# Head-by-head projection, a prefix-maximum scan and earlier attention units in the third mixer

## The reference

```python
z = u @ w_in                                  # q, k, v, o: 4 heads x 128 each; i, f: 4 each; rx, ry: 512 each
logf = log_sigmoid(f); b = cumsum(logf)       # over tokens
dmat[t, s] = b[t] - b[s] + i[s]               # s <= t, else -inf
m[t] = max(b[t] + m0, max_s dmat[t, s])       # m0 = 0: the running maximum
s[t, s] = (q @ k.T) * 128**-0.5 * exp(dmat - m)
h = (s @ v) / max(|sum_s s|, exp(-m))
y_a = sigmoid(o) * h
# the other half: causal conv of width 4 over rx, two gate matmuls, a linear recurrence
a = exp(-8 * r * softplus(-lam)); hr = scan(a, sqrt(1 - a**2) * (i_gate * xc))
y_b = gelu(ry) * hr
y = concat(y_a, y_b) @ w_out
```

## Time and profile before

| | us |
|---|---|
| median of 3 runs (2483.32 to 2484.29) | 2483.36 |
| the profiled execution | 2485.89 |
| its span | 2484.1 |
| PE busy | 2389.3 (96%) |
| DVE busy | 1200.3 (48%) |
| ACT busy | 1110.6 (45%) |
| POOL busy | 1030.5 (41%) |

### The profile page before, as it was taken

How to read it: one execution, slowest core, us unless ns; L and a number is a source line. 1 busy time by engine, 2 the same in 40 slices (tenths; PEclk the granted TensorE clock), 3 DMA queues, 4 the chain that set the end, 5 groups by cost and what they waited for, 6 DMA issues and landing times.

```text
span 2484.1 us, 40506 instructions
## 1 busy us (share of the span) xinstructions
PE 2389.3 (96%) x13254; PEld 1956.0 (79%) x13254; DVE 1200.3 (48%) x2391; ACT 1110.6 (45%) x2412; POOL 1030.5 (41%) x750
## 2 busy tenths in 40 slices
PE   7999999999999989988999999999898999999998
PEld 6878787877877768666888888887766888888886
DVE  5555455554677762564444522224775424522224
ACT  5433343444555554553644533323565644523332
POOL 4444444442533324432652544443412642544442
PEclk9999999999999999988999999999999999999999
DMA  5333333332332213221431333332322431333332
GB/s 186 114 101 94 102 91 103 101 102 94 105 91 85 85 52 102 71 65 63 127 108 52 95 101 94 96 95 74 90 65 77 132 102 52 111 94 93 101 92 77
DMA packets 126066, 232.01 MB, mean 93 GB/s; under 512 B 17120, under 2 KB 17248, under 8 KB 125920
## 3 DMA queue, kind: packets, MB, share of 16 engines
q1 hardware_dynamic: 123072, 219.56, 29.7%
q10 hardware_dynamic: 2848, 10.49, 1.2%
HBM read 208.48 MB, written 2.10 MB: 85 GB/s over the span
## 4 chain that ended last, share of the span: by engine, by line
issue 53%; PE 24%; POOL 21%; ACT 1%; DVE 1%; POOLq 1%; DMA 0%; ACTq 0%; DVEq 0%; SPq 0%
PE PS L440 22%; POOL wl L411 21%; PE PS L507 1%; PE PS L519 1%; PE PS L474 0%; DMA raw<-tiles_dram 0%; POOLq L410 0%; POOLq L419 0%; ACT wh L1102 0%; DVE H L1781 0%; PE PS L514 0%; ACT work L1211 0%; ACT work L1131 0%; DVE work L1718 0%; ACT work L1254 0%
## 5 line engine op out<-in xcount | busy, mean ns | idle before, releaser
L411 POOL TENSOR_TENSOR wl<-raw,wh 128x512 fp32r<-128x512 f32 x746 | 1030.3, 1404 | 1425.9 <-ACT wh L1102 1424.6
L440 PE MATMUL PS<-uh,wh 128*128 128x512 f32 (+1 forms) x2184 | 810.3, 371 | 13.5 <-ACT work L1254 4.6
L440 PE MATMUL PS<-uh,wl 128*128 128x512 f32 (+1 forms) x2184 | 793.7, 363 | 0.0
L440 PE MATMUL PS<-ul,wh 128*128 128x512 f32 (+1 forms) x2184 | 792.6, 363 | 0.0
L1102 ACT ACTIVATE wh<-raw 128x512 fp32r<-128x512 f32 x746 | 430.5, 623 | 348.3 <-PE PS L440 280.4
L440 PEld LDWEIGHTS PS<-uh,wh 128*128 128x128 f32 x2184 | 414.8, 190 | 99.2 <-issue 15.2
L440 PEld LDWEIGHTS PS<-uh,wl 128*128 128x128 f32 x2184 | 414.2, 190 | 65.1
L440 PEld LDWEIGHTS PS<-ul,wh 128*128 128x128 f32 x2184 | 415.1, 190 | 60.8 <-issue 1.0
L440 PE MATMUL PS<-wh,hid_sb 128*128 128x512 f32 x1024 | 322.1, 396 | 0.0
L1254 ACT ACTIVATE work<-PS 128x512 f32<-128x512 f32 (+1 forms) x156 | 89.7, 575 | 339.6 <-PE PS L440 271.2
L440 PEld LDWEIGHTS PS<-wh,hid_sb 128*128 128x128 f32 x1024 | 192.4, 188 | 46.1
(11 more groups left out here) (224 smaller groups left out, 2421.6 us busy)
## 6 DMA issues: line engine op xcount, KB each, us to landing
raw<-tiles_dram SPq DMA_DIRECT2D x746, 256.0 KB, 2.7
work<-work SPq DMA_DIRECT2D x296, 64.0 KB, 2.0
gB<-post_dram ACTq DMA_DIRECT2D x8, 512.0 KB, 3.7
H<-x_dram SPq DMA_DIRECT2D x4, 512.0 KB, 6.4
H<-x_dram ACTq DMA_DIRECT2D x4, 512.0 KB, 5.0
work<-mem_dram ACTq DMA_DIRECT2D x2, 1024.0 KB, 5.8
out_dram<-H ACTq DMA_DIRECT2D x4, 512.0 KB, 2.6
cst<-consts_dram SPq DMA_DIRECT2D x1, 644.0 KB, 5.2
```

The costliest lines, as they stand in the source:

```text
L411: nc.gpsimd.tensor_tensor(w_of(wl, slot)[:, hc], raw[:, s, hc], w_of(wh, slot)[:, hc].bitcast(F32), ALU.subtract).then_inc(lo_ready, 1)
L440: last = nc.tensor.matmul(out, a, b, start=start and m == 0, stop=stop and m == 2)
```

## The change

**Tile order.** After rx comes the tile of i and f (tile 4), then ry (5 to 8), then q, k, v, o of head 0 (9 to 12), of head 1 (13 to 16), and so on. The output projection's rows are reordered so that the recurrence's half comes first (`EV_HEADS`).

**Row maxima.** m[t] is the running maximum of i[s] - b[s], raised by b[t]: one scan with `max` over the 4 rows replaces 16 masked maxima over blocks. Only the 128x128 diagonal blocks need the mask, so they are added once into `diagonals` (16 instructions), and the exponential reads E or the diagonals directly, in two instructions per unit where n > 0.

**Units inside the tiles.** After tile m, TensorE now does the scores of unit m - 11, the transposes of unit m - 12 and the values of unit m - 13, each in one PSUM bank instead of two. Both barriers are gone. The pieces of the last units lie between pieces of the output projection (`begin`), which starts with the rows that are finished; 38 of its 64 row pieces come this way. The output gate is evacuated by a tanh directly, v at half scale.

**The recurrence** keeps its work, after tiles 5, 9, 13 and 17.

```diff
-RG_AFTER = [10, 14, 18, 22]
+RG_AFTER = [5, 9, 13, 17]
+EV_HEADS = [4, 5, 6, 7, 0, 1, 2, 3]
...
+                def ml_scores(k):
+                    h, n = k // 4, k % 4
+                    pe.wait_ge(lin_evac, LIN["ev"] + 11 + 4 * h)
+                    scores(U + k, [(PS[:, 4, 0:(n + 1) * P], eq(h)[:, n * P:(n + 1) * P], ek(h)[:, 0:(n + 1) * P],
+                                    True, True)])
...
+                    if m >= 11:
+                        ml_scores(m - 11)
+                    if m >= 12:
+                        ml_transposes(m - 12)
+                    if m >= 13:
+                        ml_values(m - 13)
...
+                begin(n, u_out, EV_EARLY[0:2], MOVED_MEM)
+                pe.wait_ge(aux_taken, AUX["ev"] + 4)
+                begin(n, u_out, EV_EARLY[2:5], MOVED_MEM)
+                ml_scores(14)
+                ml_transposes(13)
+                ml_values(12)
+                begin(n, u_out, EV_EARLY[5:10], MOVED_MEM)
...
+                    if m >= 10:
+                        ml_exps(m - 10)
+                    if m >= 12:
+                        ml_pt(m - 12)
...
-                for h in range(ML_H):
-                    nc.scalar.activation(eg[h], F[:, h, :], ACT.Tanh, scale=0.5)
...
+                    v.tensor_tensor_scan(gif[0:4, :], ones4[0:4, :], gtmp[1][0:4, :], 0.0, ALU.mult, ALU.max)
...
-                def ml_weights_max(k):
...
+                            v.tensor_tensor(eD(h)[:, ns], eA[h][:, ns], maskn[:, 384:512], ALU.add)
...
+                conv(0)
+                ml_rows()
+                gelu(0)
+                rg_gates(0)
+                rg_scan(0)
...
+                ml_probs(0)
+                conv(2)
+                gelu(2)
+                ml_values_in(0)
+                ml_probs(1)
+                rg_gates(2)
+                ml_probs(2)
+                rg_scan(2)
+                ml_probs(3)
```

More of the change, by code:

```diff
@@ L906, in _ @@
[L906 to L913, removed]
@@ L914, in _ @@
-                bound()
+                    if m >= 12 and m % 4 == 0:
+                        h = m // 4 - 3
+                        pe.wait_ge(lin_evac, LIN["ev"] + m)
+                        wait(pe, aux_taken, AUX["ev"] + h)
+                        for t in range(TT):
+                            last = nc.tensor.transpose(PS[:, 7, t * P:(t + 1) * P], evt[:, t * P:(t + 1) * P], ident)
+                        last.then_inc(aux_ready, 1)
+                    if m == 11:
+                        pe.wait_ge(act_step, 4)
@@ L1456, in rg_start, with ml_pt, head_hi @@
+                def ml_pt(k):
+                    w = (k % 4 + 1) * P
+                    pt(UNIT["ev"] + k, ept(k)[:, 0:w], PS[:, 5, 0:w])
+                def head_hi(p0, p1):
+                    for p in range(p0, p1):
+                        act.wait_ge(rows_read, c.get("rows") + min(p + 1, KT - 1))
+                        nc.scalar.activation(uh[:, p, :], F[:, EV_HEADS[p], :], ACT.Copy).then_inc(uh_ready, 1)
                 def rg_start(q):
@@ L2122, in _, with gelu @@
                     v.drain().then_inc(conv_ready, 1)
+                def gelu(q):
+                    dve.wait_ge(lin_evac, L0 + 6 + q)
                     v.tensor_tensor(gel, F[:, 4 + q, :], F[:, 4 + q, :], ALU.mult)
@@ L2189, in _ @@
[L2189 to L2201 removed]
+                    v.scalar_tensor_tensor(F[:, h, :], F[:, h, :], 1.0, PS[:, 6, :], ALU.add, ALU.mult)
@@ new lines, in ml_result, with head_lo @@
+                    v.drain().then_inc(y_taken, 1)
+                def head_lo(p0, p1):
+                    for p in range(p0, p1):
+                        dve.wait_ge(uh_ready, c.add("uh"))
+                        v.tensor_tensor(ul[:, p, :], F[:, EV_HEADS[p], :], uh[:, p, :].bitcast(F32), ALU.subtract)\
+                            .then_inc(u_ready, 1)
+                step()
+                conv(0)
[3 more added lines that the diff above has]
+                rg_scan(0)
@@ new lines, in _ @@
+                conv(1)
+                gelu(1)
+                ml_diagonals()
+                rg_gates(1)
+                rg_scan(1)
+                ml_probs(0)
[7 more added lines that the diff above has]
+                ml_probs(3)
+                conv(3)
+                gelu(3)
+                ml_probs(4)
+                ml_values_in(1)
@@ new lines, in _ @@
+                ml_probs(5)
+                ml_result(0)
+                rg_gates(3)
+                ml_probs(6)
+                rg_scan(3)
+                ml_probs(7)
+                ml_probs(8)
+                ml_values_in(2)
+                ml_probs(9)
+                ml_result(1)
+                ml_probs(10)
+                ml_probs(11)
+                ml_probs(12)
+                head_lo(0, 2)
+                ml_values_in(3)
+                ml_probs(13)
+                ml_result(2)
@@ L2408, in tok, with toks @@
         out.append(("t", w, row, at))
-    def toks(w):
+    def toks(w, rows=range(4)):
         for nb in range(2):
-            for j in range(4):
+            for j in rows:
                 tok(w, 256 * j, 512 * nb)
```

258 lines of the change are left out of this document (146 added, 112 removed).

## The result

The changed kernel takes 2444.27 us (median of 4 runs, 2441.51 to 2448.54), the kernel before on the same chip 2483.82 (4 runs): a ratio of 0.9842, 95% interval 0.9826 to 0.9857, 39.5 us less. Predicted were 2452.5 and 31 less, so the forecast was 8.2 too high; 2444.27 lies just inside the lower end of the stated range (2444). The profiled execution took 2441.51, its span is 2439.7 at a mean clock of 0.992, against 2484.1 at 0.982 before.

The account below looks back on a forecast made before the run. TensorE, busy 96% of the span, was taken to bound the kernel. Base -39.1 plus waits 8.2 gave -30.9: from the profiled 2485.89 to 2455.0, the median 2.53 lower, so 2452.5 us, range 2444 to 2467.

Parts of the forecast that it names:

- The base sum: Third mixer, if TensorE never waits: -31.4 for attention, -8.2 for the convolution hole, +0.5 for tiny transposes, -39.1 us.
- the 55.0 that go: The attention stretch without tile work, between the last turned head of v and the output projection, disappears: 55.0 us.
- the 23.6 that come back: Attention matmuls returning between the tiles: 22.0 us at full clock, plus 1.6 for changing between kinds of matmul.
- the 8.2 of the hole: First gate matmuls' wait for VectorE's convolution, 4.26 us, goes, with slow clock of 1.95 and 2.0: together -8.2.
- The waits: TensorE waiting for VectorE and ScalarE in the new order: 8.2 us in sum, between 2.9 and 13.
- rival (B): The waits vanish, each bound falling low: 2447.2 us, or 2444.3 with none at all; chance 0.14.
- the main case: Waits of 4 to 14 us including some lower clock, giving 2448 to 2459 us; chance 0.62.
- units 2 and 6 (1.2 each): VectorE's work for these units stands behind the gates of recurrence blocks 2 and 3, so TensorE waits 1.2 us each.
- Rival (A): GpSimd blocks VectorE and the relay paces TensorE: 14 us more, 2466.5; chance 0.18 with what resembles it.
- The predicted -31.4: Net of the attention stretch: 55.0 us removed, 23.6 us of matmuls and changeovers added between the tiles.
- wrong, if the rhythm is 8 and more: Sign against the prediction: per-tile rhythm of 8 us and more, where 6.4 to 7.5 was expected.
- Rival (C): Slower than before: waits between tiles keep TensorE at its lower clock, up to 2487 us; chance 0.06 with other slow mishaps.

Follow-up runs that it names:

- e8: The changed kernel run again unchanged, with a second profile: 2443.9 us, ratio 0.9841.
- e5: The changed kernel with the gate matmuls of recurrence blocks 2 and 3 behind the unit's work, VectorE in that order too: 2443.6 us.
- e1: The kernel before with only the first convolution moved ahead of the row work on VectorE: 2475.8 us, ratio 0.9973.
- e10: The kernel before with both the scan and its diagonals and the first convolution ahead of the row work, heads still alone behind barriers: 2463.3 us.
- e7: The changed kernel with units 0 to 13 behind the 25 tiles and all 20 early output pieces behind the last unit: 2458.0 us.
- e2: The kernel before with scan and diagonals in place of the masked maxima, heads still alone behind the barriers: 2470.9 us.
- e6: The changed kernel with two more VectorE additions of 128x512 behind each unit, whose result nobody reads: 2448.3 us.
- e9: The changed kernel with the scan for maxima undone, masked maxima per unit on VectorE again: 2457.3 us.
- e11: The changed kernel with the value matmuls of unit m - 13 ahead of the transposes of unit m - 12: 2444.7 us.
- e12: The changed kernel with the gate matmuls of block 0 behind tile 6 instead of tile 5: 2446.9 us.

## Why the prediction was right, and where it was not

**The base sum held.** Without any wait the stage was to lose 39.1. It lost 34.7 with 4.0 of waits, so 38.7 without: the 55.0 that go, the 23.6 that come back and the 8.2 of the hole are right within 0.4 together. That closeness is in part the luck of one profile. In e8 the stage lost 33.6 with 3.7 of waits, 37.3 without, since the fall behind the broadcast, 1.5, was there again.

**The waits were half of what I took**, 4.0 for 8.2. That is the mis-sized term. The time, 2444.3, is rival (B)'s figure for no waits at all, and that is luck: there were 4.0 of waits, and 4.8 us came from outside the stage, where the prediction has nothing. Without those 4.8 the time would be 2449.1, in the main case. The 8.2 us by which the median lies under my forecast are these 4.2 and 4.8 outside the stage (below), less the 0.4 of the base and 0.5 by which the median before came out higher this time. Tile 8 (1.0), the copy of E (0.5), tile 12 (1.0) and the tail (0.5) cost nothing. The row chain took 11.5 where I had 13.7, since the maximum scan took 1.21 for my 2.2; the gelu argument took 2.0 for my 2.4 to 4.1, and the 16 diagonals 0.21 each, my lower bound, for 0.4:

```profile
1000.92 1.70 DVE L2248 TENSOR_TENSOR diagonals<-cst,maskn 128x128 f32<-128x128 f32 x8
1002.55 1.70 DVE L2248 TENSOR_TENSOR diagonals<-maskd,maskn 128x128 f32<-128x128 f32 x8
```

**The waits had two causes together.** I had put units 2 and 6 (1.2 each) down to queueing behind the gates of the recurrence. They waited 1.04 and 1.53, so the size is right. The queueing is there: the scores of unit 2 were made by 1027.5, and VectorE began its product at 1032.60, behind the gates. But it would still have been in time, had it not then been held in instructions on one column that take 0.16 elsewhere. VectorE at unit 6, and GpSimd at that moment:

```profile
1066.46 0.57 DVE L2259 SCALAR_TENSOR_TENSOR stat<-stat 128x1 f32<-128x1 f32 x1
1067.12 1.14 DVE L2262 TENSOR_TENSOR stat<-stat 128x1 f32<-128x1 f32 x1
```

```profile
1065.69 2.55 POOL L420 TENSOR_TENSOR wl<-raw,wh 128x512 fp32r<-128x512 f32 x2 [10.23 <-ACT wh L1148]
```

1067.12 + 1.14 is 1068.26, GpSimd's 1065.69 + 2.55 is 1068.24. The two stretched instructions are 0.41 and 0.98 too long, 1.39 of the wait of 1.53. At unit 2 the same instruction took 1.14 and at unit 3 1.17, so by these rows about 3 of the 4.0 us would have gone without GpSimd. The Trainium skill (SBUF — State Buffer, Who interferes with whom) says that a VectorE instruction with two SBUF inputs contends with a GpSimd instruction that reads SBUF, and the trace agrees. Rival (A) had the right mechanism with 14 us too much, because a meeting costs only where TensorE is about to ask: at unit 7 the same instruction took 1.17 again, in units 9 and 11 the scaling (L2266) is 1.1 and 0.9 too long, and nobody waits. Without the queueing the waits go as well: in e5, where units 2 and 6 come ahead of the gates, they meet GpSimd no more and do not wait. So each of the two was needed for the waits of units 2 and 6; no run takes GpSimd's part away alone.

**The 8.2 of the convolution hole was right in sum and half wrong in cause.** I took both slow pieces of clock, 1.95 and 2.0, as the wait's. The five-microsecond windows of the kernel before show two falls, one at the wait and one behind the broadcast at 1015.04, with full clock between them:

```profile
1005.00:1010.00 5.00, 4.00 (x7) 1.87 (x8) 2.65 (x5) 0.38 (x1) 0.00 (x0) 0.66 0.09 34
1010.00:1015.00 5.00, 5.00 (x23) 3.91 (x21) 3.08 (x6) 4.01 (x7) 1.03 (x1) 1.00 0.00 0
1015.00:1020.00 5.00, 5.00 (x15) 2.50 (x15) 3.41 (x4) 3.66 (x5) 3.89 (x3) 0.99 0.35 106
1020.00:1025.00 5.00, 5.00 (x17) 3.98 (x16) 4.63 (x5) 0.00 (x0) 2.50 (x2) 0.67 0.34 107
```

In e1 and e10 the wait is gone and the second fall remains, deeper. So only the wait's 4.26 and the first slow piece, 1.95, go by moving the convolution; the second, 2.0, stands behind the broadcast. It is missing in the first profile of the changed kernel and there again in e8 and five of its other variants. What decides is open.

**Where the 39.5 come from** the prediction did not ask, and a reader might take it for the placement. By the medians: scan and convolution together some 20, the barriers with the new tile order and gate places 5.3, and both placements 14.0 (e7 to e8). Undone alone, the output pieces among the last units cost 7.4 and the units between the tiles 4.3. The scan alone is 12.2 in the old order and 13.3 in the new. The predicted -31.4 sets the whole old stretch, maxima, barriers and all, against the new matmuls. It is right as a sum and cannot tell these parts.

**The rest.** The profiled spans differ by 44.4, 9.7 more than the stage: 2.4 ahead of it and 7.3 behind it, in code that the change doesn't touch. What lies behind the stage took 1289.4 in the kernel before and 1281.0 to 1286.0 in the 13 other profiles, e1 and e2 with the same code among them. So the median fell by 4.8 more than the stage; the profiled kernel before was slower there than any other, at a clock of 0.95 in the window above. Whether that is chance of that execution or goes with this kernel's timing stays open.

**What would show it.** The windows, the first gate matmuls, the clock of 1.00 and tile 8 came as written. The waits came at units 1, 2, 4 and 6, and also 3. The bound "wrong, if the rhythm is 8 and more" was badly set: loaded periods last 8.3 to 9.0 at full clock (one 7.5), because the gate matmuls add 1.74 to some, a turn of v 0.44 to others, and a wait to most. Rival (C) did not come: waits of up to 1.53, among tiles, left the clock at 1.00. In e6 and e9, with 2.2 and 2.8 of waits within one period, it read 0.87 and 0.83 in single windows.

No version beat the changed kernel: e5 and e11 lie within its scatter.

## What to carry to other kernels

Before units are moved between tiles, see what makes them slow when they stand alone: here the shorter chain, the earlier convolution and the new order without barriers gave some 25 us with the units still alone, the placement 14. Extra work on a half-busy engine was cheap behind the result that another engine waits for (26 us for 4.4), and 13 us of other work in front of it cost 13; try the place before you go by the busy share. Price the waits with the lower bounds of the rows for engines that have the moment to themselves, and look at the tiny instructions for the meeting with GpSimd. And take a second profile of the same kernel before a fall of the clock or a small wait is put down to an edit: here it unmade one theory.

## What the runs showed of the hardware

The granted clock fell without any wait. In e1 and e10 it read 0.54 and 0.50 in a 5-us window, and in e12 0.77, all in a TensorE that was 100% busy, at or right behind four broadcast matmuls from 4 rows. Such a fall stands in 11 of 14 profiles, with one tile or two between the gate matmuls and the broadcast. One program had it in one profile (0.78) and not in another (1.00). Of the two levels, 1.2 and 2.4 GHz, these means hold both: in e12 a tile's matmuls take 0.63 there and 0.39 elsewhere.

At units 2, 3 and 6 two VectorE instructions on one column, 0.16 us alone, lasted 0.48 to 0.58 and 1.14 to 1.17 beside GpSimd, and the second ended with GpSimd's within 0.02.

A prefix scan over 4x512 lasted 1.21 alone (maxima) and 2.13 to 2.14 beside GpSimd (maxima in e12, sums in the changed kernel). Over 128x512 it lasted 1.23 alone and 2.15 beside GpSimd (at 1069.97 and 988.29 in the changed kernel).
